# Retention queries and gates by seven products in one stretch, and the next head's keys ahead of the scores in the middle heads

## What is computed

```python
proj = u @ w_in                                  # u: normed tokens, 528 x 1024
rq, rk, rv, rg, aq, ak, av, iq, ik, iw, g_ret, g_att = split(proj)
rq = rope(rq); rk = rope(rk) * 256 ** -0.5       # rotation by position
yr = retention(rq, rk, rv)                       # per head: (q k^T * decay) v, each head normed
yr = (silu(rg) * yr) @ w_ret_out                 # 2048 -> 1024
merged = sigmoid(g_ret) * yr + sigmoid(g_att) * ya
mixer = merged @ w_mix_out
```

## Time and profile before

| | us |
|---|---|
| median of 3 runs | 1926.14 |
| lowest, highest | 1925.92, 1926.17 |
| the profiled execution | 1926.5 |
| its span, first to last instruction | 1924.2 |
| TensorE matmuls busy | 1905.3 (99%) |
| VectorE, ScalarE, GpSimd busy | 1182.2, 988.1, 1016.6 |
| from the last `ao` matmul to the first `mx` matmul | 1072.74 to 1532.97 |

### The profile page before, as it was taken

How to read it: one execution, slowest core, us unless ns; L and a number is a source line. 1 busy time by engine, 2 the same in 40 slices (tenths; PEclk the granted TensorE clock), 3 DMA queues, 4 the chain that set the end, 5 groups by cost and what they waited for, 6 DMA issues and landing times.

```text
span 1924.2 us, 31665 instructions
## 1 busy us (share of the span) xinstructions
PE 1905.3 (99%) x11974; PEld 1677.7 (87%) x11974; DVE 1182.2 (61%) x2140; ACT 988.1 (51%) x1746; POOL 1016.6 (53%) x1100
## 2 busy tenths in 40 slices
PE   9999999999999999999999999999999999999998
PEld 6788777899999998789998888888888789999996
DVE  7845776877777757985442353334334367777765
ACT  5634454667676656434443252333334357767663
POOL 6432212588487475553333444454444568858554
PEclk9999999999999999999999999999999999999999
DMA  5221111222333333222221312232222222323332
GB/s 198 88 66 45 45 34 34 75 90 89 112 108 102 107 121 107 73 96 67 67 66 52 119 55 94 77 98 83 83 77 77 88 99 80 118 89 121 104 106 88
DMA packets 49653, 168.36 MB, mean 87 GB/s; under 512 B 6368, under 2 KB 8544, under 8 KB 49504
## 3 DMA queue, kind: packets, MB, share of 16 engines
q1 hardware_dynamic: 46576, 160.85, 25.1%
q10 hardware_dynamic: 2928, 5.51, 0.8%
HBM read 164.24 MB, written 2.10 MB: 86 GB/s over the span
## 4 chain that ended last, share of the span: by engine, by line
PE 92%; DVE 6%; ACT 1%; issue 1%; DMA 0%; POOL 0%; DVEq 0%; ACTq 0%
PE slot L2502 90%; DVE qkv L1726 1%; DVE x_lo L2266 0%; PE slot L2971 0%; DVE xt L2258 0%; DVE x_lo L1972 0%; PE slot L2687 0%; DVE qkv L1723 0%; DVE xt L2005 0%; PE slot L2652 0%; DVE slot L1720 0%; DMA small<-small_in 0%; DVE square L2023 0%; DVE h L2000 0%; DVE xt L1679 0%
## 5 line engine op out<-in xcount | busy, mean ns | idle before, releaser
L3049 POOL TENSOR_TENSOR w_lo<-w_raw,w_hi 128x256 fp32r<-128x256 f32 x744 | 600.1, 841 | 717.0 <-ACT w_hi L985 709.5
L2502 PE MATMUL slot<-x_hi,w_hi 128*128 128x264 f32 (+2 forms) x1384 | 469.4, 339 | 1.1 <-DVE x_lo L2266 0.7
L2502 PE MATMUL slot<-x_hi,w_lo 128*128 128x264 f32 (+2 forms) x1384 | 456.8, 330 | 0.0
L2502 PE MATMUL slot<-x_lo,w_hi 128*128 128x264 f32 (+2 forms) x1384 | 455.9, 329 | 0.0
L3055 POOL TENSOR_TENSOR w_lo<-w_raw,w_hi 128x512 fp32r<-128x512 f32 x168 | 218.4, 1311 | 151.8 <-ACT w_hi L1060 149.4
L2502 PEld LDWEIGHTS slot<-x_hi,w_hi 128*128 128x128 f32 x1384 | 260.3, 188 | 34.2 <-issue 7.6
L2502 PEld LDWEIGHTS slot<-x_lo,w_hi 128*128 128x128 f32 x1384 | 260.2, 188 | 25.2
L2502 PEld LDWEIGHTS slot<-x_hi,w_lo 128*128 128x128 f32 x1384 | 260.5, 188 | 24.0 <-issue 1.4
L985 ACT ACTIVATE w_hi<-w_raw 128x1024 fp32r<-128x1024 f32 x189 | 197.3, 1052 | 142.9 <-PE slot L2502 135.5
L2046 DVE TENSOR_TENSOR w_lo<-slot,w_hi 128x512 fp32r<-128x512 f32 x224 | 154.0, 688 | 95.2 <-ACT w_hi L1060 88.8
L2502 PE MATMUL slot<-x_sums_hi,w_hi 128*128 128x264 f32 (+1 forms) x640 | 180.7, 282 | 1.2 <-issue 1.2
(11 more groups left out here) (411 smaller groups left out, 4194.4 us busy)
## 6 DMA issues: line engine op xcount, KB each, us to landing
w_raw<-weights SPq DMA_DIRECT2D x301, 512.0 KB, 3.2
h<-x_t ACTq DMA_DIRECT2D x4, 512.0 KB, 6.7
dec<-decays ACTq DMA_DIRECT2D x4, 264.0 KB, 3.1
const<-consts SPq DMA_DIRECT2D x1, 576.0 KB, 6.6
at_rot<-rotations ACTq DMA_DIRECT2D x1, 528.0 KB, 4.1
ix_rot<-rotations ACTq DMA_DIRECT2D x1, 528.0 KB, 5.7
rt_rot<-rotations ACTq DMA_DIRECT2D x1, 528.0 KB, 3.6
w_raw<-weights SPq DMA_DIRECT2D x2, 256.0 KB, 4.3
```

The costliest lines, as they stand in the source:

```text
L2502: return nc.tensor.matmul(out, lhsT, rhs, start=start, stop=stop, skip_group_check=onto)
L3049: nc.gpsimd.tensor_tensor(w_lo[j][:, piece], w_raw[j][:, piece], w_hi[j][:, piece].bitcast(F32), ALU.subtract).then_inc(s_lo, pieces)
```

## The change

- The queries of heads 1 to 3 and all gates `rg` (22 tiles) leave the head loop. They are made by seven products in 11 jobs (`MIX_JOBS`), in one stretch after the keys and values of head 0 and ahead of its scores. The sums of tokens for it are made from `x2_hi + x2_lo` (VectorE, GpSimd, ScalarE; `t2_...`).
- A job's output is put together in `ret_y` (two halves, in turn) and stored to a DRAM tensor by SyncE's queue; a head's queries and gates are loaded back by ScalarE's queue (`queries_in`, `gates_in`). To make room, `h` and the attention output `ya` are stored to DRAM and loaded back as well.
- Values and scores get low parts of their own (`rv_lo`, `rst_lo`, where `h` was).
- The output projection `wr` of a head moves to the next head, mostly between its scores and its `ry`. The sum for the norm moves into the next head's `wide`, behind its first block.
- The keys of the next head stand ahead of the scores in heads 1 and 2, between scores and `ry` in head 0.
- Rotation of the next head's queries and keys (VectorE) and their high parts (ScalarE) stand behind the last `wr` tile and ahead of all that has to do with `ry`.
- `gr` 0 to 2 stand around the last head's norm; their sigmoids are kept. In the last block of `wide`, matmuls are sorted so that the first two token tiles are done first.

The diff, cut to its core:

```diff
@@ results() @@
+    for j in range(2):
+        add(("rk", 0, j), 1)
+    for i in range(3):
+        add(("rv", 0, i), 4 * (i == 2))
+    job_results(add, MIX)
     for hd in range(RET_H):
         if hd:
-            add(("rq", hd, 1), 1)
...
+            for i in range(3):
+                add(("rv", hd, i), 4 * (i == 2))
+            for j in range(wr_early(hd)):
+                add(("wr", hd - 1, j), j % 2)
+            if hd + 1 < RET_H:
+                for j in range(2):
+                    add(("rk", hd + 1, j), 1)
         for kt in range(NQ + 1):
             add(("rs", hd, kt))
...
+MIX_JOBS = [("rq", hd) for hd in range(1, RET_H)] + [("rg", hd, p) for hd in range(RET_H) for p in range(2)]
+def wr_early(hd):
+    return 2 if hd + 1 == RET_H else 0
@@ ScalarE @@
+            for hd in range(RET_H):
+                if hd:
+                    w_split(BLOCK["rv", hd, 2] + RING + 1)
+                    values_out(hd)
+                    w_split(BLOCK["rv", hd, 2] + RING + 3)
+                    if hd + 1 < RET_H:
+                        keys_out(hd + 1, 0)
+                        ahead(("rk", hd + 1, 1))
+                        keys_out(hd + 1, 1)
+                        w_split(BLOCK["rk", hd + 1, 1] + RING)
+                for kt in range(NQ):
+                    act.wait_ge(s_rst, 5 * hd + kt + 1)
+                    A.sig(nc.scalar.activation(ret_scores(rst_hi, kt), ...
+                if hd + 1 < RET_H:
+                    act.dma_start(dec[:], dec_dram[:, hd + 1]).then_inc(s_dec, 16)
+                    queries_in(hd + 1)
+                    if hd == 0:
+                        ahead(("rk", 1, 0))
+                        keys_out(1, 0)
+                        ahead(("rk", 1, 1))
+                        keys_out(1, 1)
+                        w_split(BLOCK["rk", 1, 1] + RING)
+                    else:
+                        w_split(BLOCK["wr", hd - 1, KD - 1] + RING)
+                    for a in range(2):
+                        rotated_high(hd + 1, a)
+                else:
+                    ahead(("gr", 0))
...
                 for d in range(4):
                     copy_out(("ry", hd, d), ret_y[:, d, :])
@@ VectorE @@
+                if hd:
+                    for j in range(wr_early(hd), KD):
+                        ret_out(hd - 1, j)
+                if hd + 1 < RET_H:
+                    rotate(hd + 1, 0)
+                    rotate(hd + 1, 1)
 
                 V.own(nc.vector.memset(square[1][:, 0:T], 0.0))
                 for d in range(4):
@@ TensorE @@
+            keys_of(0)
+            wide([("rv", 0, i) for i in range(3)])
+            for n in range(len(MIX_JOBS)):
+                for name in PRODUCTS:
+                    product(MIX, n, name, T // 2, lambda k: mix_tokens(n, name, k))
             for hd in range(RET_H):
                 if hd:
-                    dense(("rq", hd, 1), SEQ, (x2_hi, x2_lo))
...
+                    wide([("rv", hd, i) for i in range(3)], lambda: total(("rn", hd - 1), 8, T))
+                    for j in range(wr_early(hd)):
+                        ret_out(hd - 1, j)
+                    if hd + 1 < RET_H:
+                        keys_of(hd + 1)
...
+                if hd:
+                    for j in range(wr_early(hd), KD):
+                        ret_out(hd - 1, j)
+                if hd == 0:
+                    keys_of(1)
                 for i in range(3):
                     wait_evac(pe, ("rv", hd, i))
...
+            dense(("gr", 0), SEQ, (x2_hi, x2_lo))
+            total(("rn", RET_H - 1), 8, T)
+            for j in range(1, GR_EARLY):
+                dense(("gr", j), SEQ, (x2_hi, x2_lo))
+            for j in range(KD):
+                ret_out(RET_H - 1, j)
```

More of the change, by code:

```diff
@@ L251, in ffn_results @@
         add(("up", i, f), 1)
[L252 to L256, removed]
+    job_results(add, i)
     for d in range(KD):
@@ L1584, in _ @@
+            for j in range(KD):
+                ahead(("wr", RET_H - 1, j))
+            for j in range(GR_EARLY, KD):
+                ahead(("gr", j))
+                if j == GR_EARLY:
+                    x_high(2, 0, M, merged_hi)
+                sigmoid(j)
                 x_high(1, j - 1, M, merged_hi)
@@ L2751, in _, with product @@
                 out_part(j, 0, KD)
+            part_of = {"P1": 0, "P2": 1, "P3": 2, "P5": 3, "P6": 4, "P7": 5, "P4": 6}
+            token_part = {"P1": (0, 0), "P2": (1, 0), "P3": (1, 1)}
+            token_sum = {"P5": "T1", "P6": "T2", "P7": "T3", "P4": "T4"}
+            f_name = {"P1": "B11", "P2": "B2", "P3": "B2"}
+            bank_of = {"P1": "pa", "P2": "pa", "P5": "pe", "P6": "pb", "P3": "pb", "P7": "pc", "P4": "pc"}
+            seeded = {"P6": "P1", "P7": "P6", "P4": "P7"}
+            def product(i, n, name, half, source):
+                operand = OPERANDS[PRODUCTS.index(name)]
+                j, cols = operand_place(i, n, operand)
+                key, opens = (bank_of[name], i, n), name in ("P1", "P5")
+                if opens:
+                    begin(key)
+                if operand in SUMS:
+                    pe.wait_ge(s_slo, sum_at(i, n, operand))
+                else:
+                    pe.wait_ge(s_rlo, raw_low_at(i, n, operand))
+                if name in seeded:
+                    pe.wait_ge(s_seed, seed_at(i, n, seeded[name]))
+                for k in range(KD // 2):
+                    x = source(k)
+                    w = [a[j][:, cols.start + k * P:cols.start + k * P + P] for a in (w_hi, w_lo)]
+                    m = mm3(slot(key)[:, 0:half], w, x, opens and k == 0, k == KD // 2 - 1, not opens)
+                m.then_inc(s_prod, 1)
             def ffn(i, parts):
@@ L2799, in ffn @@
                 for n, job in enumerate(JOBS):
                     for name in PRODUCTS:
-                        product(n, job, name)
+                        product(i, n, name, half, lambda k: f_and_x(n, job, name, k))
                 b1 = BLOCK[("down", i, 0)]
@@ L2855, in few_rows, with wide @@
                 return m if k == KD - 1 else low()
-            def wide(keys):
+            def wide(keys, aside=None):
                 sl = [begin(k) for k in keys]
@@ L3225, in stream @@
                 w.reshape(4, P, KD, P)[:, :, j:j + 2].transpose(1, 2, 0, 3).reshape(P, 1024)))
-    for j in range(1, KD):
+    keys_of(0)
+    wide(part("rv", 0, 512))
+    for job in MIX_JOBS:
+        at = job[1] * 256 if job[0] == "rq" else job[1] * 512 + job[2] * 256
+        for j in range(2):
+            turned(part(job[0], at + j * P, P))
+    for hd in range(RET_H):
+        if hd:
+            wide(part("rv", hd * 512, 512))
+        if hd + 1 < RET_H:
+            keys_of(hd + 1)
+        if hd:
+            ret_out(hd - 1)
+    for j in range(GR_EARLY):
+        cols(part("gr", j * P, P))
+    ret_out(RET_H - 1)
+    for j in range(GR_EARLY, KD):
         cols(part("gr", j * P, P))
```

644 lines of the change are left out of this document (412 added, 232 removed).

## The result

The changed kernel takes 1946.65 us (median of 4 runs, 1945.56 to 1947.59). The kernel before took 1926.09 us in the runs beside it (1925.92 to 1926.17). The ratio is 1.0107 (95% interval 1.0089 to 1.0124): slower, by 20.6 us, and outside the predicted range of 1921 to 1943. The profiled execution took 1945.56 us, with a span of 1943.7, 19.5 longer than before.

A forecast was written before the change was run, and what follows sets the result against it. TensorE's matmuls, 1905.3 of 1924.2 us, were taken as the bound. Fewer matmuls -13.4, entry +1.5, exit +0.5, head 0 +5.2, heads 1 and 2 +15.4 gave +9.2 on 1926.1: 1935.3 us, range 1921 to 1943.

The forecast's parts named there:

- Fewer matmuls, -13.4: Retention stretch: 22 tiles (122.3 us) replaced by 11 jobs (109.2 us), with some 0.3 us of seams: 13.4 us gained.
- (d): Jobs: the seven products don't hold 0.118 us a matmul, half the gain, 1942 us; chance 0.12 together with (b).
- Entry, +1.5 (ends 0 and 5): Start of the jobs: TensorE waits 1.5 us in all, being early at the sixth and seventh products; 0 to 5.
- Rival (c): Start of the jobs: the wait takes its high end, 1938.8 us; inside the range, no chance of its own.
- Head 0, +5.2 (ends 3 and 8): Before head 0's `wide`: query load and rotation end S+29.4, TensorE arrives S+24.3 (S: scores' start); wait 5.2 us.
- Stores and loads: nothing: Retention stretch: some 20 MB of added DMA traffic, on queues with a share of 0.25, costs nothing.
- Heads 1 and 2, +15.4: Before `wide`: rotation delays the `ry` copies to E+15.8 (E: last `wr` ends); 7.7 us of wait in each head.
- The rest of each head, nothing: After the wait at `wide`: norm's sum, norm, gates and scores' decay cost nothing, the sum with 0.7 us to spare.
- (b): Norm's sum: also late, TensorE waits some 2.2 us in three heads, 1942 us; chance 0.12 together with (d).
- (a): Before `wide`: no waits arise because `ry` is copied out as promptly as before, 1914.7 us; chance 0.13.
- (e): Before `wide`: the waits are half as long as worked out, -1.1 us, 1925 us; chance 0.09.
- The moved keys don't help.: Heads 1 and 2: keys ahead of the scores don't shorten the wait, being rotated behind the last `wr` anyway; no size.

The follow-up runs named there:

- the changed kernel again: The changed kernel run once more without any edit, as reference for the follow-up runs: 1946.94 us, ratio 1.0107.
- the entry experiment: Changed kernel with the values of head 0 read out ahead of the last token sum instead of behind it: 1944.92 us, ratio 1.0096.
- the nearly filled kernel: Changed kernel with 22, 24 and 24 unread matmuls put into TensorE's waits before `wide` in the three heads: 1945.17 us, ratio 1.0097.

## Why the prediction was wrong

The direction and the place of the loss were right, and 1935.3 was 11.3 us too low. **The failed step is the sum: it priced each wait of TensorE by its length alone.** The prediction gave all matmuls the clock of the kernel before, 1.00, although it forecast waits of 5 to 8 us in a stretch in which TensorE had not waited at all. There was no term for the granted clock behind them. It is 7.6 us in the profile, of which 6.2 at the three head waits, and 5.8 when these are filled. With it alone the sum would have been 1942.9, just inside the range; the other terms were 3.3 us of idle time too low, most of it at the entry.

Point by point, by the prediction's own terms:

- **Fewer matmuls, -13.4.** Measured -14.1. The jobs with their entry wait left out took 1114.65 to 1224.89, 110.2, of which 1.4 are the low clock: 108.8 against 109.2. Seven products held 0.118 us a matmul, and (d) is out. A matmul of 512 columns was 0.231 us from start to start, 1.96 times as long.
- **Entry, +1.5 (ends 0 and 5).** Measured 3.14, and 0.78 at the first key tile for `ya_late`, and 1.4 of low clock: 5.3, above its high end. Rival (c) came true in size. The place was missed: the first product itself had to wait for VectorE's low parts of the values. ScalarE made the values' high parts only behind the last sum of tokens, which came from GpSimd at 1109.91, and VectorE's low parts followed:

```profile
1109.17 0.74 POOL L3444 TENSOR_TENSOR mix_sums<-mix_sums 128x256 f32<-128x256 f32 x1
...
1109.94 1.06 ACT L1634 ACTIVATE mix_sums_hi<-mix_sums 128x1024 fp32r<-128x1024 f32 x1 [2.82 <-POOL mix_sums L3444]
...
1111.86 1.94 ACT L1627 ACTIVATE rv<-slot 128x1024 fp32r<-128x1024 f32 x2
...
1113.38 2.35 DVE L2607 TENSOR_TENSOR rv_lo<-slot,rv 128x1024 fp32r<-128x1024 f32 x2
```

- **Exit, +0.5.** 0.2.
- **Head 0, +5.2 (ends 3 and 8).** 6.54, and 8.05 and 8.54 in the profiles of the changed kernel again and of the entry experiment. From the start of the rotation to TensorE's start it took 14.9 us, as worked out (14.2 to 14.9). What was off is the arrival of the queries, and the near hit is two errors that almost cancel. ScalarE ordered them sooner than forecast, at S+8.8 and not S+10.9 or later, but they landed late, at S+16.1 instead of S+15.2, and 1.5 later still in the next execution. The two loads of head 1's queries took 6.2 us (median) from order to landing, not 3.1; those for heads 2 and 3 took 3.4. This is where "Stores and loads: nothing" was wrong. The last job's store and the weights were on the queues as well, and the DMA share was 1.03 while the queries were on their way. That the traffic made them late is argued and not tested. DMA orders and window, kernel after:

```profile
square<-kept ACTq DMA_DIRECT2D x2, 256.0 KB, 6.2
...
1235.00:1241.00 6.00, 6.00 (x52) 6.00 (x51) 1.99 (x4) 1.56 (x2) 6.00 (x9) 1.00 1.03 379
```

- **Heads 1 and 2, +15.4.** 15.2. The chain came out link by link. These rows are head 1 of the kernel after, with E at 1322.75:

```profile
1322.95 0.69 DVE L2673 COPY yr<-slot 128x512 f32<-128x512 f32 x1 [2.06 <-PE slot L2773]
1323.75 0.69 DVE L2588 TENSOR_TENSOR xt<-square,rt_rot 128x512 f32<-128x512 f32 x1
...
1329.65 1.15 ACT L1621 ACTIVATE rqk_hi<-xt 128x512 fp32r<-128x512 f32 x2 [5.58 <-DVE xt L2594]
...
1335.78 1.18 ACT L1621 ACTIVATE rqk_hi<-xt 128x528 fp32r<-128x528 f32 x2 [4.98 <-DVE xt L2594]
1336.86 2.04 ACT L1115 ACTIVATE ret_y<-slot 128x512 f32<-128x512 f32 x4
```

  The rotation starts at E+1.0 (predicted E+0.95), the queries are done at E+6.9 (6.8), the keys at E+13.0 (12.9), the copies start at E+14.1 (14.0), and TensorE goes on at E+15.9 (15.8), 1338.67.
- **The rest of each head, nothing.** Right: VectorE's squares end at 1344.47, E+21.7 (21.6 predicted), and the norm's sum never waits, so (b) is out too. So are (a) and (e), since the waits came at full length.
- **"The moved keys don't help."** They don't help, they cost: the prediction looked at the rotation alone. Where the keys stand decides whether TensorE has work while VectorE rotates, and that was worth some 15 us, 12.4 of them idle time (7.62 to 1.42 and 7.62 to 1.41).

By terms: 3.3 more idle time (2.4 entry, 1.3 head 0, the rest -0.4) and 7.6 of clock, less 0.7 more gain, make 10.2, which takes +9.2 to the +19.4 of the profile. The median of the runs lies 1.1 above the profiled execution.

Left open: how much of the spread between the runs (2 us) is head 0's load and how much the clock at the entry. No run separates the two.

## What to carry to other kernels

In this kernel, where TensorE is busy nearly all the time, each wait of 3.8 us or more cost its length and then 1.5 to 2.4 us more as matmuls at the lower clock: put a second term beside every wait in a sum, and look at the granted clock right behind it. Before a result that begins several slots at once, ask what stands in program order ahead of the copies that free them, since TensorE waits for what of it is not covered: here `ry` covered 8.3 us of the 15.9 from E to the start of `wide`, and 7.6 were a wait. Such work belongs where an engine waits in short pieces anyway, here between tiles that come every 2.8 us, where TensorE waited no more than 0.25 us.

## What the runs showed of the hardware

- In the mixer's stretch the clock fell behind every wait of 3.8 us or more (13 of 13 in the profiles, 0.50 to 0.66 over the 5 us behind), stayed at 1.00 behind all waits of 1.3 to 1.5 us (6 of 6), and went both ways between. Behind 3.37 us it was 0.66. Behind the entry's 3.14 to 3.17 us it was 0.68 to 0.72 up to 1120.00 in six profiles and 1.00 in one. Behind 2.1 us it was 1.00 in one and 0.66 in another. Behind 2.0 us it was 0.66 twice. So in these profiles the length of a wait from 2 to 3.2 us does not settle it.
- Near the start of every profile TensorE waits 1.3 to 2.3 us for the low parts of its first weights, and the clock is 1.00 behind all eleven of these waits.
- A load of 256 KB landed in 3.4 us for the queries of heads 2 and 3, and in 6.2 us for those of head 1, with the DMA share at 1.03 from 1235 to 1241 (kernel after).
- A low stretch cost 1.4 to 2.4 us. In the nearly filled kernel it began after the restart of the matmuls: 1.5 us of matmuls at 0.23 us (clock 0.98), then 0.43 (0.50).
